# A two-layer decoder trunk on one core: the first part's convolution on three engines, and the mix and output projection placed among the rows of v

## The reference

```python
mod = (c_act @ w_ada[l] + b_ada[l])[:, None, :]
sh1, sc1, g1, sh2, sc2, g2 = jnp.split(mod, 6, axis=-1)
h = rms_norm(x) * (1.0 + sc1) + sh1
q, k, v, qi, ki, wi, cu = jnp.split(h @ w_in[l], offs, axis=-1)
...
attn = dsa_attention(q, k, v, qi, ki, wi).reshape(B, T, ATTN_WIDTH)
conv = conformer_conv(cu, conv_dw[l], conv_b[l], conv_ln_g[l], conv_ln_b[l])
mixed = jnp.concatenate([rms_norm(attn, out_g_attn[l]), rms_norm(conv, out_g_conv[l])], axis=-1)
x = x + g1 * (mixed @ w_out[l])
h2 = rms_norm(x) * (1.0 + sc2) + sh2
x = x + g2 * peer_ffn(h2, peer_wq[l], peer_sub_keys[l], peer_u[l], peer_v[l])
```

## Time and profile before

| | us |
|---|---|
| median of 3 runs (lowest, highest) | 1898.0 (1894.2, 1899.7) |
| the profiled execution, its own time | 1898.8 |
| its span, first to last instruction | 1896.8 |
| busy in it: TensorE, VectorE, ScalarE, GpSimd | 1071, 1042, 300, 977 |

### The profile page before, as it was taken

How to read it: one execution, slowest core, us unless ns; L and a number is a source line. 1 busy time by engine, 2 the same in 40 slices (tenths; PEclk the granted TensorE clock), 3 DMA queues, 4 the chain that set the end, 5 groups by cost and what they waited for, 6 DMA issues and landing times.

```text
span 1896.8 us, 20984 instructions
## 1 busy us (share of the span) xinstructions
PE 1071.0 (56%) x7558; PEld 630.1 (33%) x7558; DVE 1042.1 (55%) x2867; ACT 300.3 (16%) x851; POOL 976.5 (51%) x1072
## 2 busy tenths in 40 slices
PE   3896840784786566755486555774477550003554
PEld 2584630653462115443254114453153110000110
DVE  2312399799538018888518307789728219993000
ACT  6222100243210002342100002352010000000000
POOL 2000044553355776445435677534556777776774
PEclk8897975897797667876688787986788885556887
DMA  8547798999999999999999999997999999999998
GB/s 289 176 136 267 266 369 329 382 400 343 360 336 400 409 409 402 397 388 348 401 400 402 408 409 406 399 396 277 401 405 380 409 409 410 410 410 406 407 409 321
DMA packets 230920, 696.15 MB, mean 367 GB/s; under 512 B 23958, under 2 KB 23974, under 8 KB 230818
## 3 DMA queue, kind: packets, MB, share of 16 engines
q0 software_dynamic: 148080, 538.24, 72.5%
q1 hardware_dynamic: 82738, 156.58, 22.7%
HBM read 693.70 MB, written 1.05 MB: 366 GB/s over the span
## 4 chain that ended last, share of the span: by engine, by line
DMA 40%; PE 24%; DVE 14%; POOL 11%; issue 5%; ACT 5%; POOLq 0%; ACTq 0%; DVEq 0%
DMA rows<-in_peer_v,v_at 18%; DMA rows<-in_peer_u,u_at 8%; DMA wring<-in_w_in 8%; POOL rows L517 7%; PE ps L652 6%; DVE rows L1116 6%; PE ps L599 5%; PE ps L610 5%; POOL rows L509 4%; DMA wring<-in_w_ada 4%; ACT rows L907 2%; PE ps L575 2%; PE ps L633 1%; DMA wring<-in_w_out 1%; ACT diag_eq L907 1%
## 5 line engine op out<-in xcount | busy, mean ns | idle before, releaser
L509 POOL DMA_INDIRECT rows<-in_peer_u,u_at x512 | 480.6, 939 | 585.6 <-DVE dots L1116 254.2
L1116 DVE CUSTOM_DVE_ANT_0 rows<-rows,ps 128x1024 f32<-128x1024 f32 x512 | 601.6, 1218 | 224.5 <-DMA rows<-in_peer_u,u_at 217.0
L517 POOL DMA_INDIRECT rows<-in_peer_v,v_at x512 | 484.5, 946 | 313.2 <-PE ps L652 155.4
L652 PE MATMUL ps<-rows,spread_c 128*32 128x512 f32 x2048 | 343.9, 804 | 260.8 <-DMA rows<-in_peer_v,v_at 259.6
L599 PE MATMUL ps<-wring,hT 128*128 128x512 f32 x384 | 206.0, 692 | 74.9 <-DMA wring<-in_w_in 48.3
L652 PEld LDWEIGHTS ps<-rows,spread_c 128*32 128x32 f32 x2048 | 73.8, 129 | 504.0 <-issue 500.1
L610 PE MATMUL ps<-hT,wring 128*128 128x128 f32 x1536 | 184.5, 284 | 7.3 <-ACTq L874 7.3
L610 PEld LDWEIGHTS ps<-hT,wring 128*128 128x128 f32 x1536 | 182.2, 200 | 11.2 <-ACTq L874 8.5
L599 PEld LDWEIGHTS ps<-wring,hT 128*128 128x128 f32 x384 | 81.9, 222 | 187.2 <-issue 93.9
L907 ACT ACTIVATE diag_eq<-ident,cwT 128x128 f32<-128x128 f32 x395 | 118.3, 387 | 28.9 <-PE ps L633 27.5
L548 PE MATMUL ps<-ident,coef 128*128 128x128 f32 x4 | 1.5, 373 | 192.4 <-DVE coef L1384 192.4
(11 more groups left out here) (193 smaller groups left out, 959.8 us busy)
## 6 DMA issues: line engine op xcount, KB each, us to landing
wring<-in_w_ada SPq DMA_DIRECT2D x48, 1024.0 KB, 11.4
wring<-in_w_in SPq DMA_DIRECT2D x48, 1024.0 KB, 22.3
wring<-in_peer_wq SPq DMA_DIRECT2D x32, 1024.0 KB, 12.7
wring<-in_w_out SPq DMA_DIRECT2D x16, 1024.0 KB, 19.6
rows<-in_peer_u,u_at POOLq DMA_INDIRECT x512, 12.8
rows<-in_peer_v,v_at POOLq DMA_INDIRECT x512, 9.1
wring<-in_w_in SPq DMA_DIRECT2D x4, 288.0 KB, 23.7
out_x<-xs SPq DMA_DIRECT2D x2, 512.0 KB, 4.7
```

The source lines that it names most:

```text
L509: pool.indirect_dma_start(row(n), None, u_rows, bass.IndirectOffsetOnAxis(ap=u_at[:, p % 2, k:k + 1], axis=0)).then_inc(row_landed[n % SLO ...
L517: pool.indirect_dma_start(row(n), None, v_rows, bass.IndirectOffsetOnAxis(ap=v_at[:, p % 2, tok:tok + 1], axis=0)).then_inc(row_landed[n % ...
L652: ins = pe.matmul(ps[32 * g:32 * g + 32, YB + q, :], spread_c[:, g, a, :], row(n)[:, q * 512:q * 512 + 512], start=a == 0, stop=a == 31)
L1116: dve.tensor_tensor_reduce(out=row(n), in0=row(n), in1=h2_shown, scale=1.0, scalar=0.0, op0=ALU.mult, op1=ALU.add, accum_out=dots[:, k:k + ...
```

## The change

The convolution of part 0 is split by channel groups: group 0 stays on TensorE with 31 diagonals (four batches), groups 1 and 2 are 31 multiply-adds each on VectorE, group 3 is 31 scalings and 30 additions on GpSimd. The three accumulators lie in row slot 4, are turned by TensorE into the convolution's bank behind the modulation "mix", and the layer norm follows there.

In all parts the two branch norms and silu (and for p > 0 the convolution's layer norm, which ScalarE serves by copying the bank to `hb`), the transposes of the mix and the output projection move from `first(p)` to `second(p)`. For p > 0 they then stand behind the coefficients of p - 1, with steps of `v_to` between them. The modulation blocks (1, 0) and (1, 1) move from "out" to "tail" of part 0, and `FIRST_DOTS` becomes (0, 14, 30, 46).

```diff
-CONV_BETWEEN = [(1, 2, 3), (4, 5), (6,), (7,)]
-FIRST_DOTS = (0, 10, 22, 34)
+FIRST_DOTS = (0, 14, 30, 46)
...
-    (0, "out"): [(1, 0), (1, 1)],
-    (0, "tail"): [(1, 2), (1, 3)],
+    (0, "tail"): [(1, 0), (1, 1), (1, 2), (1, 3)],
...
         def tap_diag(p, n, j):
 
-            if p == 0 and n < SLOTS:
+            if p == 0:
                 return rows[:, n, j * P:(j + 1) * P]
             return diags[:, n % 2, j, :]
+        def batches_to(p, n):
+            return n if p == 0 else 4 + 16 * (p - 1) + n
+        acc = rows[:, 4, 0:512].rearrange("p (j t) -> p j t", j=CT)
+        tap_tmp = rows[:, 5, 0:2 * P].rearrange("p (b t) -> p b t", b=2)
...
+            pool.wait_ge(cw_ready, 1)
+            pool.wait_ge(glu_done, 1)
+            ct = CT - 1
+            o = acc[:, ct, :]
+            seq_(pool.tensor_scalar(o, hc[:, ct, 0:P], cwT[:, ct, 0:1], cwT[:, ct, TAPS:TAPS + 1], ALU.mult, ALU.add))
+            for i in range(1, TAPS):
+                tmp = tap_tmp[:, i % 2, :]
+                seq_(pool.tensor_scalar(tmp, hc[:, ct, i:i + P], cwT[:, ct, i:i + 1], None, ALU.mult))
+                seq_(pool.tensor_tensor(o, o, tmp, ALU.add), conv_pool if i == TAPS - 1 else None)
...
                 if p == 0:
                     proj(("v", p), hT)
                     conv(p, 0)
+                    conv(p, 1)
...
-                    if p == 0:
-                        for pair in CONV_BETWEEN[2 * i]:
-                            conv(p, pair)
...
                 values(ns[-1])
                 ada(p, "mix")
-                pe.wait_ge(mixed_ready, p + 1)
-                for q in range(2):
-                    turn4(("mT", p, q), [hb[:, (4 * q + i) * P:(4 * q + i + 1) * P] for i in range(4)])
-                pe.wait_ge(mixedT_ready, 2 * (p + 1))
-                for b in range(2):
-                    proj(("out", p, b), hT)
-                ada(p, "out")
+                if p == 0:
+                    pe.wait_ge(conv_dve, 2)
+                    pe.wait_ge(conv_pool, 1)
+                    pe.wait_ge(diag_used, 4)
+                    for ct in range(1, CT):
+                        ins = pe.transpose(ps[:, CONV_BANK, ct * P:(ct + 1) * P], acc[:, ct, :], ident[:, :])
+                    ins.then_inc(conv_full, 1)
...
-                v_to(p - 1, 1)
+                v_to(p - 1, 2)
+                pe.wait_ge(mixed_ready, p + 1)
+                for q in range(2):
+                    turn4(("mT", p, q), [hb[:, (4 * q + i) * P:(4 * q + i + 1) * P] for i in range(4)])
+                pe.wait_ge(mixedT_ready, 2 * (p + 1))
+                for b in range(2):
+                    proj(("out", p, b), hT)
+                    v_to(p - 1, 3 + b)
+                ada(p, "out")
+                v_to(p - 1, 5)
                 pe.wait_ge(h2_ready, p + 1)
...
-                v_to(p - 1, 2)
+                v_to(p - 1, 6)
...
-                    v_to(p - 1, 4 + 2 * b_)
+                    v_to(p - 1, 8 + 2 * b_)
...
                 if p == 0:
-                    make_diags(p, 0, 1, 2, 3, 4)
-                    ada(p, "pre", 5)
+                    act.sem_inc(cw_ready, 1)
+                    make_diags(p, 0, 1, 2, 3)
+                    ada(p, "pre")
...
                 if p:
-                    silu()
+                    act.wait_ge(conv_full, p + 1)
+                    act.copy(hb[:, AW:D], ps[:, CONV_BANK, :]).then_inc(conv_taken, 1)
...
+                act.wait_ge(silu_in, p + 1)
+                act.activation(hb[:, AW:D], hb[:, AW:D], ACT.Silu).then_inc(silu_done, 1)
                 for q in range(2):
                     evac_scaled(("mT", p, q), q, mixedT_ready, gcol)
                 ada(p, "out")
...
                 if p:
-                    conv_norm()
                     more_dots(3)
...
                 if p == 0:
-                    conv_norm()
-                dve.wait_ge(silu_done, p + 1)
-                rsqrt(half_mean_square(hv, CW, gy[:, :]), 1)
-                seq_(ts(hv, hv, rs[:, 0:1], None, ALU.mult))
+                    dve.wait_ge(cw_ready, 1)
+                    for i in range(TAPS):
+                        for ct in (1, 2):
+                            o, w = acc[:, ct, :], cwT[:, ct, i:i + 1]
+                            if i == 0:
+                                seq_.lag(ts(o, hc[:, ct, 0:P], w, cwT[:, ct, TAPS:TAPS + 1], ALU.mult, ALU.add))
+                            elif i < TAPS - 1:
+                                seq_.lag(stt(o, hc[:, ct, i:i + P], w, o, ALU.mult, ALU.add))
...
+                    conv_norm(0)
...
-                rsqrt(half_mean_square(ha, AW, gy[:, :]), 1)
-                seq_(ts(ha, ha, rs[:, 0:1], None, ALU.mult), mixed_ready)
...
+            def join(p):
+                if p:
+                    conv_norm(p)
+                for n, cols in enumerate((slice(0, AW), slice(AW, D))):
+                    if n:
+                        dve.wait_ge(silu_done, p + 1)
+                    rsqrt(half_mean_square(hb[:, cols], AW, gy[:, :]), 1)
+                    seq_(ts(hb[:, cols], hb[:, cols], rs[:, 0:1], None, ALU.mult), mixed_ready if n else None)
```

63 lines of the change are left out of this document (30 added, 33 removed).

## The result

The changed kernel takes 1865.38 us (median of 4 runs, 1862.16 to 1870.65), the kernel before 1898.85 (4 runs, 1894.2 to 1901.67). The ratio is 0.9821, interval 0.9803 to 0.9838: 33.5 us faster, where the forecast was 58. The profiled execution took 1870.65 us, its span is 1868.8, against 1896.8 before: 28.0 us of span. One execution of one variant further down, g2_late, took 3375.36 us where its other five took 2051.73 to 2077.74; it is left out of that variant's numbers, and the record shows no cause for it.

The account below looks back on a forecast made before the run. After about 240 us the kernel was taken as DMA-bound, losing time only where the engines idle. Terms 32 + 8 + 6 + 5 + 8 = 59 us off 1898 gave 1840 us; own range 1815 to 1866, overall range 1808 to 1874.

Parts of the forecast that it names:

- The opening, 32 us: Part 0 up to the first gather: shorter ScalarE and TensorE work brings that gather from 239.92 to near 208 us.
- This counts in full: First gather: its 32 us all reach the total, since the queue has fetched about the same bytes by then.
- cost nothing on VectorE, since they would follow anyhow: Part 0's selections: twelve more dots (46, not 34) free slots sooner, 15.7 us of transfer, at no VectorE cost.
- The same queue has fetched about the same bytes by then: Up to the first gather: reason given for counting the 32 us in full, with wq's weights one place earlier.
- 240:350, 8 us: Idle transfer time at 240:350 and 440:502, 23.2 us: early dots and removed norms take back 8 (0 to 20).
- 502:570, 6 us: Stretch around part 0's coefficients' spread: join and output projection lie beside gathering, taking back 6 of 8.4 us idle.
- Parts 2 and 3, 5 and 8 us: Dips at 850:870 and 1270:1320: norms leave VectorE, taking back 5 of 7.4 and 8 of 15.4 us.
- Only the opening counts: Rival: only part 0's opening gains, later dips keep their size; 1866 to 1876 us, chance 0.17.
- The twelve early dots delay everything behind them: No-change rival: early dots in part 0 wait for rows, giving back the opening's 32 us; 1898 us, chance 0.03.
- GpSimd's chain in part 0: Slower rival: accumulator transposes wait for GpSimd's convolution; slower than before past 1.9 us an instruction; chance 0.03.
- The last sign of being wrong: A v stretch in which TensorE stands at the transposes of the mix with all 13 slots full.
- 400 GB/s throughout: Sign of being right: this throughput throughout what answers to the 502:570 stretch.

Follow-up runs that it names:

- g2_late: Changed kernel with the two modulation blocks that make g2, in parts 1 and 3, put behind the output projection; 2069.60 us, ratio 0.985, on a slower chip.
- dots_34: Changed kernel with the old counts of dots in the first part's choice (0, 10, 22, 34); 1853.89 us, ratio 0.9752.
- opening_alone: First part as in the change, parts 1 to 3 in the order of the kernel before; 1892.61 us, ratio 0.9964.
- opening_34: First part as in the change but with dot counts 0, 10, 22, 34, parts 1 to 3 in the old order; ratio 0.9887, slower chip.
- ada_back: Changed kernel with modulation blocks (1,0) and (1,1) behind the first part's output projection again; 1868.46 us, ratio 0.9827.
- join_alone: Kernel before with only norms, silu and output projection moved behind the coefficients in parts 1 to 3; 1872.04 us, ratio 0.9854.
- v_ahead: Changed kernel with four more v rows taken ahead of each step of the join; 2049.15 us, ratio 0.9763, slower chip.
- mix_split: Changed kernel with the scale's two modulation blocks of the first part behind its output projection; ratio 0.9819, slower chip.
- three: Changed kernel with 34 dots, four more v rows ahead of each join step, and the first part's scale blocks behind its output projection; ratio 0.9742, slower chip.
- dots_24: Changed kernel with dot counts 0, 8, 16, 24 in the first part's choice; ratio 0.984, slower chip.

## Why the prediction was half right

Faster was right, and the time fell inside the range, near its slow end. The own range of the likeliest case (1815 to 1866) was reached only at its edge, and by luck as much as by reasoning: the opening was valued far too high and the moved join far too low.

**The opening, 32 us: measured 20.9 at the first gather.** The missing 11 us are lost by 149.1, where the last modulation should have ended at 138.5: the first projection came at 44.91, not 41 (its last weights landed at 36.8 for 36, but what follows them took 8.1 us, not 5), and the last modulation started at 126.26, not 120.5, and took 22.9 us, not 18. From there to the gather it went as worked out (69.9 us against 69.5). That is a term mis-sized. GpSimd begins at 90.45 instead of 86, its 30 scalings take 0.65 us each and its 30 additions 0.46, with 0.1 between them, where I took 0.4, and it ends at 129.6 instead of 110. The cover held, since TensorE came to the accumulators at 149.12, and that price cost nothing.

**"This counts in full": the step that failed.** With it failed the sentence of the next part that twelve more dots "cost nothing on VectorE, since they would follow anyhow". They would, but behind the choice, and the next part hangs on the choice. From the first gather to the end of the choice it took 83.9 us before, 100.6 after, and 83.6 in dots_34. So 16.7 of the 20.9 us were spent there, opening_alone kept 6.9, and dots_34 got them back; opening_34, on another chip, points the same way. The chain of work of the changed kernel shows what hangs on it (start, duration, piece):

```profile
318.55 1.13 DVE rows L1131
320.93 1.22 DVE hb L1095
325.69 1.51 ACT hT L893 x4
...
328.92 8.84 PE ps L629 x56
337.78 11.69 DMA wring<-in_w_in
349.51 5.41 PE ps L618 x8
354.94 27.99 DMA wring<-in_w_in
```

The last dot of the choice, the norm of part 1, its transposes, and then projections paced by their weights, on to the attention and the coefficients. These were expected near 462 and came at 488.8 (473.8 in dots_34).

"The same queue has fetched about the same bytes by then" failed too: up to the first gather 186 x 0.243 + 33 x 0.129 = 49.5 MB were moved, against 206 x 0.221 + 34 x 0.243 = 53.8 before. By ada_back this cost nothing that the times show, because the deferred weights fill the later dip.

**240:350, 8 us.** The dip closed nearly, but for another reason than the dots: dots_34 has no dip with 34, ada_back has it with 46. It is the moved modulation weights.

**502:570, 6 us: the largest error of size.** join_alone, which holds this term and those of parts 2 and 3, measures 27.5. The wait of 15.17 and the 10.5 us of norms (9.3 of which join_alone shows ahead of the coefficients) both stood in the prediction, in two different terms, and were valued by the idle transfer time of the stretch behind them instead of by the date of the spread. On this chip the time behind the spread did not change: from it to the end of the span 1379.5 us before, 1379.3 after (1896.8 - 517.3; 1868.8 - 489.5), 1378.5 in join_alone, 1380.8 in opening_alone, 1381.7 in dots_34 and 1379.5 in ada_back. **Parts 2 and 3, 5 and 8 us,** were accordingly 0 by that count. The dips shrank (343 GB/s for 279 in the one of part 3), and the spreads inside came earlier by more than the first: the second by 38.2 us (958.8 to 920.6), the third by 40.7 (1381.7 to 1341.0); but the fourth only by 29.5 (1726.6 to 1697.1). One reason may be that the output projection's weights now also have to be carried behind the spread (by the mean throughput 547 MB there in join_alone, 541 before); that was argued and not tested. "At most 2 us to the spread" was right (0.8), "400 GB/s throughout" behind it was not: 285 in 470:530.

**The rivals.** "Only the opening counts" names a time (1866 to 1876) near the measured one, but its mechanism is refuted: the opening alone is worth 6.9 us, the move 27.5. "The twelve early dots delay everything behind them" was the no-change rival with a chance of 0.03. Its mechanism is what happened to the opening, at 16.7 us and not 32, and mostly by VectorE's own time: twelve dots, one every 1.14 us, are 13.7 us, and in 219:300 it was busy 74.62 of 81. The rest is about what it waited for rows: 3.2 us in four waits from 245 to 252 us, for 0.3 before and 0.5 in dots_34. So the rival's own reason, rows that come late, had a small part. GpSimd's chain in part 0 did not lead. The last sign of being wrong showed in part: TensorE stands 5.02 us for VectorE's norms ahead of the transposes of the mix (to 500.4), but the ring is full only behind them, from 503 us on.

The sum in the prediction's form: opening 20.9, dots -16.7, moved join 25.8, together 30.0 at the spread; measured 27.8. Of the rest, 2.2 us, 1.9 are what join_alone already had at the end of the choice, which its move does not explain.

Left open: why on the slower chips the spread follows the choice by 182 to 218 us (v_ahead, mix_split, three, dots_24), where with the moved join it took 167 to 172 on the first. Between the two dots_34 moves 66 MB at 384 GB/s, three 68 MB at 332: transfers that are slower there are an obvious candidate, but no run separates them from engines that ask for less. And behind the first spread the slower chips take 1534 to 1562 us, so there its date does not tell the time as it does on the first.

## What to carry to other kernels

Value a change in a staged kernel by the date of the handover that the rest hangs on, here the coefficients' spread: list that date in both kernels first, and count an idle stretch only behind it. List the later handovers too: here the third spread gained 40.7 us and the span 28.0, and v_ahead won behind a first spread that came no earlier. Work that "has to be done anyhow" is not free ahead of a decision on which the next stage waits; ask of each edit made to close a dip what it stands in front of. Nor is it free behind all the rest: the ten dots that dots_24 took from the choice came last, after VectorE had stood idle. Where the DMA engines bound the kernel, loads that depend on nothing can fill the stretch in which the gathers are known to stall (ada_back against the changed kernel: 292 and 391 GB/s).

## What the runs showed of the hardware that I had not expected

GpSimd's instruction with one tile and a scalar for each partition (128x128) takes longer than its addition of two tiles, and only the first is slower while VectorE runs its multiply-adds on the accumulators, from 111 us on:

```profile
109.64 0.60 POOL L517 TENSOR_SCALAR rows<-hc,cwT 128x128 f32<-128x128 f32 x1
110.33 0.45 POOL L518 TENSOR_TENSOR rows<-rows 128x128 f32<-128x128 f32 x1
...
112.16 0.71 POOL L517 TENSOR_SCALAR rows<-hc,cwT 128x128 f32<-128x128 f32 x1
112.95 0.46 POOL L518 TENSOR_TENSOR rows<-rows 128x128 f32<-128x128 f32 x1
```

0.60 becomes 0.71, 0.45 stays 0.46. VectorE's own two chains show no loss: 58 multiply-adds took 19.45 us, 0.335 each, and five around GpSimd's end 0.328 each; but no run has them without GpSimd at their side. From 112 to 129 us both engines work nearly without a gap. The rule of the Trainium skill, "SBUF — State Buffer", section "Who interferes with whom", that such a pair excludes each other, shows here at most as 0.11 us on one of two kinds of instruction, over the 14 of them from there to its end some 1.5 us, and not on the chain. The additions read SBUF too and are not slower, so this trace bears the rule out only in part, and that VectorE causes the 0.11 us is inferred from the same moment alone.

The same kernel differs by 10% between chips: 1899.5 us on one, 2096.8 and 2101.2 on two others. The 696.14 MB are moved at a mean of 372 GB/s by the changed kernel, and on one of the slower chips so by v_ahead:

```profile
DMA packets 230920, 696.14 MB, mean 341 GB/s; under 512 B 23958, under 2 KB 23974, under 8 KB 230818
```

It is not only the mean: from 600 to 800 us the changed kernel moves 403 GB/s and v_ahead 365, and the mean granted clock of TensorE is 0.766 and 0.716. Each of the eight variants timed on the slower chips is faster there than the kernel before, by 1.1 to 3.0%; since none was timed on both kinds of chip, whether a gain keeps its size is not shown.
